# Forgetting attention: copies behind the exponent, rests a step later in every second head, and the causal mask added by VectorE in the score bank

## The chip, the cores and the metric

The kernel runs on one core of one Trainium2 chip. Its engines work side by side, each on its own list of instructions: TensorE (PE in the rows; PEld is its weight load), VectorE (DVE), ScalarE (ACT), GpSimd (POOL) and SyncE (SP), which issues DMAs. They meet at semaphores only: an instruction adds to one when it is done, another engine waits until it has reached a value. The metric is the device time of one execution in microseconds (us); less is better.

## The reference, cut to what matters

The program is two transformer blocks over 512 tokens of 1024 features. The change lies in the forgetting attention of the second block: 8 heads of 64, causal, with the running sum F of log-sigmoids of a gate added to the scores.

```python
F = jnp.cumsum(jax.nn.log_sigmoid(f_logit.astype(jnp.float32)), axis=1).transpose(0, 2, 1)
...
s = jnp.einsum('bhqd,bshd->bhqs', q_blk, k, preferred_element_type=jnp.float32)
s = s + F_blk[..., None] - F[:, :, None, :]
s = jnp.where(pos_blk[:, None] >= k_pos[None, :], s, -jnp.inf)
p = jax.nn.softmax(s, axis=-1).astype(v.dtype)
return jnp.einsum('bhqs,bshd->bqhd', p, v)
```

Everything is computed in float32 to the accuracy of float32: a product is made of three matmuls, of the high part of each operand and of the "rest" (the operand less its rounded high part).

## The kernel before, in words

**Order of the work.** Each engine's order is written out by hand; nothing is scheduled. After the projections (`pe_mix_in`), the attention runs in 32 steps, 8 heads h times 4 blocks qt of 128 queries; step i is head i // 4, block i % 4, and its scores have n = 128, 256, 384 or 512 columns, as block qt sees only keys up to itself. I call the last 128 of these columns the own block; only there does the mask act.

**One step, engine by engine.**

- TensorE (`pe_fox`, L2556) makes the scores of step i in one of three banks (`score_bank`): a matmul of query and key (L2571), a bf16 matmul that adds the mask in the own block (L2572: identity times a matrix with 0 and -1e30), and a matmul with the rests and with F (L2573). Then it transposes the probabilities of step i-3 (L2581, n/128 of them), at a head's first step also multiplies the values of head h-2 (`fox_out`, L2600, 8 of them in a trace row), and last it does a piece of another job: three k-tiles of three matmuls (L2308 to L2310) of the delta-rule projections ("conv products").
- VectorE (`dve_fox`, L2604) takes the negated maximum of each row of scores (L2625), then `inverse_sum` (L2619) of the exponent's sums. Between these it works on the projection tiles: it reads a tile when it is ready (L2338), adds three convolution taps (L2348), and gates it (L2360). For the next head it makes the query's rest (L2438) and the key's rest (L2442), before the change in blocks 0 and 1 of every head from head 1 on.
- ScalarE (`act_fox`, L2673) in step i: copies the turned probabilities of step i-4 from a bank to SBUF (L2682, the "copy"), scales the probabilities of step i-1 (L2686), takes the exponent of step i (L2692), and then serves the projection tiles (L2366, L2371), and rounds queries and keys of the coming head (L2425 to L2449).
- GpSimd (`pool_fox`) splits weights for the projections and builds masks; among them, earlier, the causal mask CM (`pool_causal_mask`).

**What waits for what, around the change.** The transposes of step j = i-3 write one of two banks, so they wait for the copy of step j-2 = i-5 (`fx_pt`). They also wait for the scaled probabilities of step j (`fx_p`). Scores of step i wait for the exponent of step i-3 (`fx_e`), since three banks take turns. A head's first step waits for both rests of that head (`fx_rest`) and for the rounded operands. The exponent waits for the maximum (`fx_nm`), the scaling for the inverse sum (`fx_r`), and VectorE's inverse sum for the exponent.

**Tiles of the projections.** Twelve tiles end in steps 2, 5, 7, 10, 13, 15, 18, ..., three per two heads. A tile is read in that step, its taps are added one step later, and it is gated three steps later. Where VectorE has both in a step, the read or gate stands ahead of what follows, as the code below shows.

Of the kernel before, what the change touches and what calls it, by code (L numbers as in the profile page):

```python
# [20 lines left out]
BF16 = mybir.dt.bfloat16  # L21
# [5 lines left out]
P = 128  # L27
# [118 lines left out]
def _members(kind, *parts):  # L146
# [20 lines left out]
    [("b_xc_lo", KB), ("row_sel", 4), ("f_rows", 1), ("gb_split", 4), ("go_with_q", TOK), ("column_half", 1)], [("b_xc_hi", KB), ("row_ones", 2), ("mask_b", 2), ("f_placed", 4)],  # L167
# [56 lines left out]
def build(nc, dram, out, phases=PHASES, dump=None):  # L224
# [3 lines left out]
    with ctx:  # L228
        base = 16640

        def place(name, at_kib, shape, dt=F32):
            return nc.alloc_sbuf_tensor_at(name, [P] + shape, dt, offset=base + int(at_kib * KIB))
# [1955 lines left out]
        IDENT_B = place("ident_b", ZAT + 28, [P], BF16)  # L2188
        CAUSAL_B = place("causal_b", ZAT + 28.25, [P], BF16)
# [186 lines left out]
        def act_mix_in(act):  # L2376
# [7 lines left out]
            nc.scalar.activation(IDENT_B[:, :], IDENT[:, :], ACT.Copy).then_inc(S("mask_b"), 1)  # L2384
            act.wait_ge(*due("causal", 2))
            nc.scalar.activation(CAUSAL_B[:, :], CM, ACT.Copy).then_inc(S("mask_b"), 1)

# [168 lines left out]
        def pe_fox(pe):  # L2556
            pe.wait_ge(*due("fk", PFQ.rounds - 1))
            pe.wait_ge(*due("mask_b", 2))
            for i in range(STEPS + 2):
                h, qt = divmod(i, TOK)  # L2560
                if i < STEPS:
                    if qt == 0:
                        pe.wait_ge(*due("fx_rowc", h + 1))
                        pe.wait_ge(*due("fx_rest", 2 * h + 2))
                        pe.wait_ge(*due("fx_rounded", query_again(h)))
                        if h == 0:
                            pe.wait_ge(*due("f_placed", 4))
                    n, ps = (qt + 1) * P, score_bank(i)
                    if i >= 3:
                        pe.wait_ge(*due("fx_e", i - 2))  # L2570
                    nc.tensor.matmul(ps[:, 0:n], FX_Q[h % 2][:, qt * P:n], FX_K[h % 2][:, 0, 0:n], start=True, stop=False)  # L2571
                    nc.tensor.matmul(ps[:, n - P:n], IDENT_B[:, :], CAUSAL_B[:, :], start=False, stop=False)  # L2572
                    nc.tensor.matmul(ps[:, 0:n], FX_QF[:, h % 2, qt * P:n], FX_K[h % 2][:, 1, 0:n], start=False, stop=True).then_inc(S("fx_s"), 1)  # L2573
# [30 lines left out]
        def dve_fox(dve, step):  # L2604
            MXC, SUMC = SC[:, 0:32], SC[:, 32:64]

# [13 lines left out]
            for i in range(STEPS + 3):  # L2620
                h, qt = divmod(i, TOK)
                if i < STEPS:
                    n = (qt + 1) * P
                    dve.wait_ge(*due("fx_s", i + 1))
                    nc.vector.reduce_max(MXC[:, i:i + 1], score_bank(i)[:, 0:n], axis=AX.X, negate=True).then_inc(S("fx_nm"), 1)  # L2625
# [14 lines left out]
                if 1 <= h and h + 1 < FOXH and qt == 0:  # L2640
                    dve_query_rest(dve, h + 1)
                elif 1 <= h and h + 1 < FOXH and qt == 1:
                    dve_key_rest(dve, h + 1)
# [29 lines left out]
        def act_fox(act):  # L2673
            MXC, SUMC = SC[:, 0:32], SC[:, 32:64]
            for i in range(STEPS + 3):
                h, qt = divmod(i, TOK)
                for j in turned_at(i - 1) if i else []:
                    jh, jq = divmod(j, TOK)
                    act.wait_ge(*due("fx_t", j + 1))
                    if jh >= 2 and jq == 0:  # L2680
                        act.wait_ge(*due("fx_o", jh - 1))
                    nc.scalar.activation(FPT[:, jh % 2, 0:jq + 1, jq * P:(jq + 1) * P], PS[2 + j % 2][:, 0:(jq + 1) * P].rearrange("p (k q) -> p k q", q=P), ACT.Copy).then_inc(S("fx_pt"), 1)  # L2682
# [4 lines left out]
                if i < STEPS:  # L2687
# [4 lines left out]
                    nc.scalar.activation(FP[:, i % 3, 0:n], score_bank(i)[:, 0:n], ACT.Exp, bias=MXC[:, i:i + 1], accum_out=SUMC[:, i:i + 1]).then_inc(S("fx_e"), 1)  # L2692
                started, ended = tile_at(i, 0), tile_at(i, 2)
# [1099 lines left out]
```

## Time and profile before

| | us |
|---|---|
| median of 3 runs (lowest to highest) | 1822.17 (1821.49 to 1822.44) |
| profiled execution, its own time | 1823.4 |
| its span, first to last instruction | 1821.7 |

| engine | busy us | share of the span |
|---|---|---|
| PE matmul | 1786.6 | 98% |
| DVE | 1175.9 | 65% |
| ACT | 740.6 | 41% |
| POOL | 1310.0 | 72% |

The two stretches of [rows 2] begin and end with the first score matmul of a head (1053.09 is step 4, 1080.78 step 12, 1109.08 step 20). The 32 steps start at 1042.35 (first score matmul) and the last of them ends at about 1155 us of the span. A busy PE is one with a matmul in flight: starts, not durations, tell what one matmul costs the next. A row of the timeline has the start, the duration and the operation, and in brackets how long its engine stood idle before it and who released it.

### The profile page before, as it was taken

The page shows a single profiled execution, that of the slowest core. Times are in us where ns is not written, and L with a number is a line of the kernel's source. Part 1 is how long each engine was busy: PE and PEld are TensorE (multiplying, and loading weights), DVE is VectorE, ACT ScalarE, POOL GpSimd, SP SyncE. Part 2 cuts the span into 40 slices and gives each one's busy share as a digit, 9 for nine tenths or more (in the row PEclk, how much of TensorE's full clock was granted, in tenths as well). Part 3 has the DMA queues.
Part 4 walks back from the last instruction along what each step waited for, and adds up shares of the span by engine and source line. Part 5 has one row for each costly group of instructions (what it writes and reads, how often), then busy time and mean ns, then how long its engine had stood idle before and what let it go on. Part 6 is the DMA issues. An engine that isn't in the chain of part 4 may idle for free.

```text
span 1821.7 us, 28330 instructions
## 1 busy us (share of the span) xinstructions
PE 1786.6 (98%) x10180; PEld 1523.0 (84%) x10180; DVE 1175.9 (65%) x1775; ACT 740.6 (41%) x1386; POOL 1310.0 (72%) x1188
## 2 busy tenths in 40 slices
PE   9999999999999999999999999999999999999998
PEld 7788888878878799998888867798876778999886
DVE  7976664249974798877017777664454189888631
ACT  5521111137762466652014277453413256565001
POOL 8976666767777798877667865453772688888775
PEclk9999999999999999999999999999999999999999
DMA  7022223232123323234222211101321222322421
GB/s 280 1 101 84 92 92 139 92 128 88 73 76 109 139 94 116 94 116 183 95 93 105 105 58 56 61 26 47 116 95 45 93 109 80 113 102 108 168 98 69
DMA packets 26014, 179.36 MB, mean 98 GB/s; under 512 B 2864, under 2 KB 2992, under 8 KB 6960
## 3 DMA queue, kind: packets, MB, share of 16 engines
q1 hardware_dynamic: 24176, 168.31, 25.8%
q10 hardware_dynamic: 1728, 9.58, 1.4%
q8 instruction: 70, 1.15, 0.2%
q14 instruction: 40, 0.33, 0.1%
HBM read 171.58 MB, written 6.29 MB: 98 GB/s over the span
## 4 chain that ended last, share of the span: by engine, by line
PE 82%; DVE 8%; ACT 4%; issue 3%; POOL 3%; DMA 1%; ACTq 0%; DVEq 0%; POOLq 0%
PE bank L484 12%; PE bank L485 12%; PE bank L486 12%; PE bank L1432 6%; PE bank L1433 6%; PE bank L1434 6%; PE bank L1904 2%; PE bank L1902 2%; PE bank L1903 2%; PE bank L522 1%; POOL weights_lo L762 1%; PE bank L524 1%; PE bank L523 1%; DVE x_mixed_lo L1608 1%; PE bank L3183 1%
## 5 line engine op out<-in xcount | busy, mean ns | idle before, releaser
L376 POOL TENSOR_TENSOR weights_lo<-raw_weights,weights_hi 128x512 fp32r<-128x512 f32 (+4 forms) x400 | 543.1, 1358 | 39.8 <-ACT weights_hi L395 7.4
L374 POOL TENSOR_SCALAR weights_hi<-raw_weights 128x512 fp32r<-128x512 f32 (+4 forms) x376 | 259.5, 690 | 314.3 <-PE bank L486 170.6
L484 PE MATMUL bank<-x_hi,weights_hi 128*128 128x512 f32 x688 | 271.5, 395 | 0.2
L486 PE MATMUL bank<-x_lo,weights_hi 128*128 128x512 f32 x688 | 267.9, 389 | 0.0
L485 PE MATMUL bank<-x_hi,weights_lo 128*128 128x512 f32 x688 | 267.8, 389 | 0.0
L484 PEld LDWEIGHTS bank<-x_hi,weights_hi 128*128 128x128 f32 x688 | 129.2, 188 | 28.1 <-POOL weights_lo L376 0.8
L486 PEld LDWEIGHTS bank<-x_lo,weights_hi 128*128 128x128 f32 x688 | 129.1, 188 | 27.1
L485 PEld LDWEIGHTS bank<-x_hi,weights_lo 128*128 128x128 f32 x688 | 129.2, 188 | 27.0 <-issue 1.0
L1434 PE MATMUL bank<-x_lo,weights_hi 128*128 128x256 f32 x432 | 122.4, 283 | 0.0
L1474 POOL TENSOR_TENSOR weights_lo<-temps,weights_hi 128x512 fp32r<-128x512 f32 x72 | 107.5, 1512 | 4.7 <-ACT weights_hi L1511 4.7
L1474 POOL TENSOR_TENSOR weights_lo<-raw_weights,weights_hi 128x512 fp32r<-128x512 f32 x72 | 97.6, 1358 | 13.3 <-ACT weights_hi L1511 13.0
L1432 PE MATMUL bank<-x_mixed_hi,weights_hi 128*128 128x256 f32 x288 | 81.8, 284 | 2.0 <-DVE bank L1697 2.0
L1434 PEld LDWEIGHTS bank<-x_lo,weights_hi 128*128 128x128 f32 x432 | 83.2, 193 | 0.0
L1432 PE MATMUL bank<-x_hi,weights_hi 128*128 128x256 f32 x288 | 82.0, 285 | 0.5 <-ACT temps L1523 0.5
L1433 PE MATMUL bank<-x_hi,weights_lo 128*128 128x256 f32 x288 | 81.8, 284 | 0.0
L1433 PE MATMUL bank<-x_mixed_hi,weights_lo 128*128 128x256 f32 x288 | 81.5, 283 | 0.0
L1474 POOL TENSOR_TENSOR weights_both<-temps,weights_lo 128x512 fp32r<-128x512 f32 x36 | 49.9, 1386 | 33.9 <-ACT weights_lo L1511 33.9
L1628 DVE TENSOR_TENSOR temps<-raw_weights 128x512 f32<-128x512 f32 x71 | 72.4, 1020 | 0.0
L484 PE MATMUL bank<-ffn_y_hi,weights_hi 128*128 128x512 f32 x176 | 68.8, 391 | 0.0
L486 PE MATMUL bank<-ffn_y_lo,weights_hi 128*128 128x512 f32 x176 | 68.5, 389 | 0.0
L485 PE MATMUL bank<-ffn_y_hi,weights_lo 128*128 128x512 f32 x176 | 68.5, 389 | 0.0
L1902 PE MATMUL bank<-weights_hi,ffn_y_hi 128*128 128x512 f32 x176 | 68.5, 389 | 0.0
(588 smaller groups left out, 5186.3 us busy)
## 6 DMA issues: line engine op xcount, KB each, us to landing
raw_weights<-in_ffn_seven SPq DMA_DIRECT2D x36, 1024.0 KB, 4.7
raw_weights<-in_a_ug SPq DMA_DIRECT2D x16, 1024.0 KB, 4.8
raw_weights<-in_b_in SPq DMA_DIRECT2D x12, 1024.0 KB, 4.7
raw_weights<-in_ffn_down SPq DMA_DIRECT2D x12, 1024.0 KB, 4.7
raw_weights<-in_ffn_down SPq DMA_DIRECT2D x7, 1408.0 KB, 6.1
raw_weights<-in_a_out SPq DMA_DIRECT2D x8, 1024.0 KB, 4.8
raw_weights<-in_ffn_up SPq DMA_DIRECT2D x8, 1024.0 KB, 4.8
raw_weights<-in_b_out SPq DMA_DIRECT2D x8, 768.0 KB, 4.2
```

What stands on the lines that cost most here:

```text
L374: nc.gpsimd.tensor_scalar(hi, raw, 1.0, 0.0, ALU.mult, ALU.add).then_inc(S("units_hi"), 1)
L376: nc.gpsimd.tensor_tensor(lo, raw, hi.bitcast(F32), ALU.subtract).then_inc(units_ready, 1)
L484: nc.tensor.matmul(ps, wh, xh[:, k, :], start=k == 0, stop=False)
L485: nc.tensor.matmul(ps, wl, xh[:, k, :], start=False, stop=False)
L486: last = nc.tensor.matmul(ps, wh, xl[:, k, :], start=False, stop=k == last_k)
L1432: nc.tensor.matmul(out, wh, xh(k), start=opens and k == 0, stop=False, skip_group_check=True)
L1433: nc.tensor.matmul(out, wl, xh(k), start=False, stop=False, skip_group_check=True)
L1434: last = nc.tensor.matmul(out, wh, xl(k), start=False, stop=k == 3, skip_group_check=True)
L1474: nc.gpsimd.tensor_tensor(RING_LO[p], source_of(r, p), RING_HI[p].bitcast(F32), ALU.subtract).then_inc(S("seven_lo"), 1)
L1628: nc.vector.tensor_tensor(sum_of(p), x, y, op).then_inc(S("seven_sums"), 1)
L1902: nc.tensor.matmul(bank, Y_H[:, k, tok], wh, start=k == 0, stop=False)
L1903: nc.tensor.matmul(bank, Y_H[:, k, tok], wl, start=False, stop=False)
```

## The change

Four things are done, all inside the attention:

1. The bf16 mask matmul of each of the 32 steps is gone, and with it the bf16 copies of identity and mask (two ScalarE copies, made some 45 us ahead of the first step).
2. VectorE instead adds the mask CM, in float32, to the own block in the score bank (128 x 128), ahead of the row maximum; the maximum waits for this add through the new semaphore count `fx_masked`. All scores of a bank are then complete as before.
3. ScalarE makes the copy of turned probabilities right behind the exponent: in step i that of step i-3, where before it was made at the head of step i+1.
4. In heads 2, 4 and 6 the rests of the next head are made one block later, in blocks 1 and 2 (`later` = 1); in heads 1, 3 and 5 they stay in blocks 0 and 1.

```diff
@@ act_mix_in
-            nc.scalar.activation(IDENT_B[:, :], IDENT[:, :], ACT.Copy).then_inc(S("mask_b"), 1)
-            act.wait_ge(*due("causal", 2))
-            nc.scalar.activation(CAUSAL_B[:, :], CM, ACT.Copy).then_inc(S("mask_b"), 1)
@@ pe_fox
-            pe.wait_ge(*due("mask_b", 2))
...
                     nc.tensor.matmul(ps[:, 0:n], FX_Q[h % 2][:, qt * P:n], FX_K[h % 2][:, 0, 0:n], start=True, stop=False)
-                    nc.tensor.matmul(ps[:, n - P:n], IDENT_B[:, :], CAUSAL_B[:, :], start=False, stop=False)
                     nc.tensor.matmul(ps[:, 0:n], FX_QF[:, h % 2, qt * P:n], FX_K[h % 2][:, 1, 0:n], start=False, stop=True).then_inc(S("fx_s"), 1)
@@ dve_fox
+            dve.wait_ge(*due("causal", 2))
...
+                    own_block = score_bank(i)[:, n - P:n]
                     dve.wait_ge(*due("fx_s", i + 1))
+                    nc.vector.tensor_tensor(own_block, own_block, CM, ALU.add).then_inc(S("fx_masked"), 1)
+                    dve.wait_ge(*due("fx_masked", i + 1))
                     nc.vector.reduce_max(MXC[:, i:i + 1], score_bank(i)[:, 0:n], axis=AX.X, negate=True).then_inc(S("fx_nm"), 1)
...
-                if 1 <= h and h + 1 < FOXH and qt == 0:
+                later = 1 - h % 2
+                if 1 <= h and h + 1 < FOXH and qt == later:
                     dve_query_rest(dve, h + 1)
-                elif 1 <= h and h + 1 < FOXH and qt == 1:
+                elif 1 <= h and h + 1 < FOXH and qt == 1 + later:
                     dve_key_rest(dve, h + 1)
@@ act_fox
             for i in range(STEPS + 3):
                 h, qt = divmod(i, TOK)
-                for j in turned_at(i - 1) if i else []:
-                    ... (wait for fx_t and fx_o, copy to FPT)
                 if 1 <= i <= STEPS:
...
                     nc.scalar.activation(FP[:, i % 3, 0:n], score_bank(i)[:, 0:n], ACT.Exp, bias=MXC[:, i:i + 1], accum_out=SUMC[:, i:i + 1]).then_inc(S("fx_e"), 1)
+                for j in turned_at(i):
+                    ... (the same waits and the same copy)
```

**ScalarE around the exponent of step 13** (head 3, block 1: the row with 128x256 from a bank). Before:

```order
L2434 ACTIVATE fox_q_with_f<-fox_q 64x512
L2682 ACTIVATE fox_pt<-bank 128x2x128
L2686 ACTIVATE fox_p<-fox_p,scratch_cols 128x128
L2692 ACTIVATE fox_p,scratch_cols<-bank,scratch_cols 128x256
L2366 ACTIVATE temps<-gdn_xb_a,vecs 128x512
L2449 ACTIVATE fox_q_with_f<-fox_f_queries,head_selectors 64x512
L2430 ACTIVATE fox_k_even<-fox_k 64x512
L2682 ACTIVATE fox_pt<-bank 128x3x128
L2686 ACTIVATE fox_p<-fox_p,scratch_cols 128x256
```

The same stretch after the change, with its new line numbers (L2684 is the exponent, L2690 the copy, L2678 the scaling):

```order
L2429 ACTIVATE fox_q_with_f<-fox_q 64x512
L2678 ACTIVATE fox_p<-fox_p,scratch_cols 128x128
L2684 ACTIVATE fox_p,scratch_cols<-bank,scratch_cols 128x256
L2690 ACTIVATE fox_pt<-bank 128x3x128
L2364 ACTIVATE temps<-gdn_xb_a,vecs 128x512
L2444 ACTIVATE fox_q_with_f<-fox_f_queries,head_selectors 64x512
L2425 ACTIVATE fox_k_even<-fox_k 64x512
L2678 ACTIVATE fox_p<-fox_p,scratch_cols 128x256
```

The copy of three tiles (step 10) has moved from behind the work for tile and head to right behind the exponent; the number of copies is the same.

**VectorE in head 2, from the taps of step 8 to the maximum of step 11** (`fox_q_odd` is the query's rest for head 3, `fox_k_odd` the key's). Before:

```order
L2348 SCALAR_TENSOR_TENSOR temps<-gdn_xb_a,vecs,temps 128x512 x3
L2438 TENSOR_TENSOR fox_q_odd<-fox_q,fox_q_odd 64x512
L2625 TENSOR_REDUCE scratch_cols<-bank 128x1
L2619 RECIPROCAL scratch_cols<-scratch_cols 128x1
L2442 TENSOR_TENSOR fox_k_odd<-fox_k,fox_k_odd 64x512
L2625 TENSOR_REDUCE scratch_cols<-bank 128x1
L2360 SCALAR_TENSOR_TENSOR gdn_qkv_t<-gdn_qkv_t,temps 128x512
L2619 RECIPROCAL scratch_cols<-scratch_cols 128x1
L2338 TENSOR_TENSOR gdn_xb_b<-bank,rms_rows 128x512
L2625 TENSOR_REDUCE scratch_cols<-bank 128x1
```

The same stretch after the change (L2620 is the mask's add, L2622 the maximum, L2613 the inverse, L2433 and L2437 the rests):

```order
L2346 SCALAR_TENSOR_TENSOR temps<-gdn_xb_a,vecs,temps 128x512 x3
L2620 TENSOR_TENSOR bank<-bank,masks 128x128
L2622 TENSOR_REDUCE scratch_cols<-bank 128x1
L2613 RECIPROCAL scratch_cols<-scratch_cols 128x1
L2433 TENSOR_TENSOR fox_q_odd<-fox_q,fox_q_odd 64x512
L2620 TENSOR_TENSOR bank<-bank,masks 128x128
L2622 TENSOR_REDUCE scratch_cols<-bank 128x1
L2358 SCALAR_TENSOR_TENSOR gdn_qkv_t<-gdn_qkv_t,temps 128x512
L2613 RECIPROCAL scratch_cols<-scratch_cols 128x1
L2336 TENSOR_TENSOR gdn_xb_b<-bank,rms_rows 128x512
L2437 TENSOR_TENSOR fox_k_odd<-fox_k,fox_k_odd 64x512
L2620 TENSOR_TENSOR bank<-bank,masks 128x128
```

An add stands ahead of each maximum; the query's rest has gone behind the maximum and inverse of step 9, and the key's rest behind everything of step 10, which makes it the last piece ahead of step 11.

## Rows read from the trace of the kernel before

**Rows 1.** The page: the span, and the chain that ended last by engine.

```profile
span 1821.7 us, 28330 instructions
PE 82%; DVE 8%; ACT 4%; issue 3%; POOL 3%; DMA 1%; ACTq 0%; DVEq 0%; POOLq 0%
```

**Rows 2.** Stretches: length, PE, PEld, DVE, ACT, POOL busy (count), granted clock, DMA.

```profile
1053.09:1080.78 27.69, 25.04 (x125) 18.79 (x124) 22.65 (x37) 18.10 (x44) 18.18 (x20) 1.00 0.15 50
1080.78:1109.08 28.30, 27.41 (x134) 19.93 (x132) 19.51 (x36) 21.76 (x50) 15.98 (x20) 1.00 0.17 64
```

**Rows 3.** Waits of TensorE, 1042 to 1158: total us, times, longest.

```profile
PE bank L2581 <- ACT fox_pt L2682: 4.6, 5, 1.6
```

**Rows 4.** Waits of TensorE behind the attention, 1158 to 1330.

```profile
PE bank L2799 <- DVE temps L2804: 0.2, 1, 0.2
```

**Rows 5.** Groups by form, 1042 to 1158: count, busy us, mean ns, idle before.

```profile
L2572 PE MATMUL bank<-causal_b,ident_b 128*128 128x128 bf16 x32 | 7.4, 230 | 0.0
```

**Rows 6.** Timeline of TensorE and its weight loads, step 15.

```profile
1092.72 0.40 PE L2571 MATMUL bank<-fox_k_odd,fox_q_odd 128*128 128x512 f32 x1
1092.95 0.10 PEld L2572 LDWEIGHTS bank<-causal_b,ident_b 128*128 128x128 bf16 x1 [0.28 <-issue]
1092.96 0.23 PE L2572 MATMUL bank<-causal_b,ident_b 128*128 128x128 bf16 x1
1092.96 0.20 PEld L2573 LDWEIGHTS bank<-fox_k_odd,fox_q_with_f 128*128 128x128 f32 x1
1093.00 0.48 PE L2573 MATMUL bank<-fox_k_odd,fox_q_with_f 128*128 128x512 f32 x1
1093.31 0.27 PE L2581 MATMUL bank<-ident,fox_p 128*128 128x128 f32 x1
```

**Rows 7.** Timeline of TensorE: transposes that waited in steps 11, 12 and 20.

```profile
1078.59 0.30 PE L2581 MATMUL bank<-ident,fox_p 128*128 128x128 f32 x1 [1.57 <-ACT fox_pt L2682]
1082.08 0.41 PE L2581 MATMUL bank<-ident,fox_p 128*128 128x128 f32 x2 [0.89 <-ACT fox_pt L2682]
...
1110.02 0.41 PE L2581 MATMUL bank<-ident,fox_p 128*128 128x128 f32 x2 [0.54 <-ACT fox_pt L2682]
```

**Rows 8.** Timeline of ScalarE: exponent 9, the copy, exponents 10 and 18.

```profile
1075.72 0.47 ACT L2692 ACTIVATE fox_p<-bank,scratch_cols 128x256 f32<-128x256 f32 x1 [2.73 <-DVE scratch_cols L2625]
...
1077.98 0.47 ACT L2682 ACTIVATE fox_pt<-bank 128x384 f32<-128x384 f32 x1
...
1078.88 0.56 ACT L2692 ACTIVATE fox_p<-bank,scratch_cols 128x384 f32<-128x384 f32 x1
...
1107.18 0.56 ACT L2692 ACTIVATE fox_p<-bank,scratch_cols 128x384 f32<-128x384 f32 x1
```

**Rows 9.** Timeline of VectorE in steps 8 to 10.

```profile
1073.70 1.66 DVE L2438 TENSOR_TENSOR fox_q_odd<-fox_q,fox_q_odd 64x512 fp32r<-64x512 f32 x1
1075.28 0.41 DVE L2625 TENSOR_REDUCE scratch_cols<-bank 128x1 f32<-128x256 f32 x1
...
1076.52 0.69 DVE L2442 TENSOR_TENSOR fox_k_odd<-fox_k,fox_k_odd 64x512 fp32r<-64x512 f32 x1
1077.24 0.56 DVE L2625 TENSOR_REDUCE scratch_cols<-bank 128x1 f32<-128x384 f32 x1
...
1079.57 0.16 DVE L2619 RECIPROCAL scratch_cols<-scratch_cols 128x1 f32<-128x1 f32 x1 [0.69 <-ACT fox_p L2692]
1080.00 0.69 DVE L2338 TENSOR_TENSOR gdn_xb_b<-bank,rms_rows 128x512 f32<-128x512 f32 x1 [0.27 <-issue]
```

**Rows 10.** Groups of VectorE by form, 1042 to 1152.

```profile
L2625 DVE TENSOR_REDUCE scratch_cols<-bank 128x1 f32<-128x512 f32 x8 | 5.5, 684 | 0.7 <-PE bank L2573 0.7
L2338 DVE TENSOR_TENSOR gdn_xb_a<-bank,rms_rows 128x512 f32<-128x512 f32 x6 | 4.1, 690 | 0.9 <-PE bank L2310 0.8
L2438 DVE TENSOR_TENSOR fox_q_odd<-fox_q,fox_q_odd 64x512 fp32r<-64x512 f32 x3 | 3.6, 1212 | 0.1
L2625 DVE TENSOR_REDUCE scratch_cols<-bank 128x1 f32<-128x128 f32 x8 | 2.2, 280 | 0.0
```

More of the change, by code:

```diff
@@ L166 @@
     *(_members(kind, ("fx", FOXH * TOK), ("ma", MH * TOK)) for kind in ("s", "nm", "e", "p", "t", "pt")),
-    [("b_xc_lo", KB), ("row_sel", 4), ("f_rows", 1), ("gb_split", 4), ("go_with_q", TOK), ("column_half", 1)], [("b_xc_hi", KB), ("row_ones", 2), ("mask_b", 2), ("f_placed", 4)],
+    [("b_xc_lo", KB), ("row_sel", 4), ("f_rows", 1), ("gb_split", 4), ("go_with_q", TOK), ("column_half", 1)], [("b_xc_hi", KB), ("row_ones", 2), ("f_placed", 4), ("fx_masked", FOXH * TOK)],
     [("beta_tanh", 1), ("a_exp", 1), ("rows_exp", 1)],
@@ L2187, in build @@
         HEAD_SEL = place("head_selectors", 207.53125, [FOXH])
-        IDENT_B = place("ident_b", ZAT + 28, [P], BF16)
-        CAUSAL_B = place("causal_b", ZAT + 28.25, [P], BF16)
         FP = place("fox_p", ZAT + 2, [3, SEQ])
@@ L2676, in act_fox @@
                 h, qt = divmod(i, TOK)
-                for j in turned_at(i - 1) if i else []:
[L2678 to L2682, printed above, removed]
                 if 1 <= i <= STEPS:
@@ L2692, in act_fox @@
                     nc.scalar.activation(FP[:, i % 3, 0:n], score_bank(i)[:, 0:n], ACT.Exp, bias=MXC[:, i:i + 1], accum_out=SUMC[:, i:i + 1]).then_inc(S("fx_e"), 1)
+                for j in turned_at(i):
+                    jh, jq = divmod(j, TOK)
+                    act.wait_ge(*due("fx_t", j + 1))
+                    if jh >= 2 and jq == 0:
+                        act.wait_ge(*due("fx_o", jh - 1))
+                    nc.scalar.activation(FPT[:, jh % 2, 0:jq + 1, jq * P:(jq + 1) * P], PS[2 + j % 2][:, 0:(jq + 1) * P].rearrange("p (k q) -> p k q", q=P), ACT.Copy).then_inc(S("fx_pt"), 1)
                 started, ended = tile_at(i, 0), tile_at(i, 2)
```

## The prediction

> **What bounds the kernel now.** The page first: the chain that ended last runs through TensorE for 82% of the 1821.7 us span, VectorE and ScalarE have 8% and 4% [rows 1]. So this edit pays only as far as TensorE's stream gets shorter or waits less. Next the stretches of the attention: in steps 4 to 11 TensorE is busy 25.04 of 27.69 us and VectorE 22.65, in steps 12 to 19 it is 27.41 of 28.30 and 19.51, at the full granted clock in both [rows 2]. The reader is to see a TensorE with few holes, and a VectorE that has little room in the first of the two stretches. The table of waits names the holes: five times, 4.6 us in all, transposes waited for the copy of turned probabilities, the longest 1.6 us [rows 3]. The timeline puts one in step 11 (1.57), one in step 12 (0.89) and one in step 20 (0.54) [rows 7]; the other two, in steps 7 and 28, share what is left, 4.6 - 3.0 = 1.6 us. Behind the attention TensorE waits next to nothing for VectorE (0.2 us) [rows 4].
>
> Why the copy is late in step 11: exponent 9 starts at 1075.72, having waited 2.73 us for its maximum; ScalarE then serves tile and head and comes to the copy at 1077.98, and the transposes start at 1078.59 [rows 7, 8]. The maximum was late because VectorE first made the query's rest, 1.66 us from 1073.70 on [rows 9].
>
> **Part 1, the mask matmul removed.** 32 are gone. Their busy time is 230 ns each, 7.4 us in all [rows 5], but matmuls overlap, and starts count. In step 15 L2572 starts at 1092.96 and L2573 at 1093.00: 0.04 us. L2573 itself then holds on for 0.31 until the next start, where L2571 of the same 512 columns took 0.24 (1092.72 to 1092.96) [rows 6]; its duration is 0.08 longer too (0.48 against 0.40). I read this as a weight load (0.20) that the short mask matmul cannot cover. Without the mask matmul it lies beside L2571: at 512 and 384 columns all of it (0.04 + 0.08 = 0.12 saved), at 256 about half (0.09, an interpolation), at 128 columns none (0.04). Mean 0.09 us per step. Bounds: 0.04, the start distance alone, and 0.23, the busy time. For the 20 steps from 12 on: 1.9 us, between 0.8 and 4.6. The two ScalarE copies that go lie some 45 us earlier, where ScalarE idles: nothing.
>
> The Trainium skill, page "TensorE: Matmul & The Clock Gate", Part 3, The mechanism, says that a weight load overlaps with matmuls in flight only where the row groups differ; for full-height tiles the mask's own load (0.10) would then be exposed too, and each step would give some 0.15. The trace disagrees: the 0.20 load of L2573 starts at 1092.96 and its matmul 0.04 later [rows 6]. By the page the 20 steps would give 3.0 instead of 1.9.
>
> **Part 2, the add on VectorE.** No row shows a 128 x 128 add in a bank. The maximum of 128 columns takes 280 ns and of 512 columns 684; a tensor-tensor of bank and SBUF at 512 columns takes 690, much the same [rows 10]. So I take 0.28 for the add, plus 0.04 until the dependent maximum starts, an estimate: 0.32 us per step, 10.2 us of VectorE in 32 steps, 2.6 per two heads. Bounds: 0.15 (the maximum's fixed part, 280 less 128 columns at (684 - 280)/384 ns) and 0.69. VectorE's load in steps 12 to 19 rises from 19.5 to 22.1 of some 27 us; below TensorE, but all of the add lies on the chain score, maximum, exponent, inverse sum. Queued behind it on VectorE are reads, taps and rests, for which ScalarE and TensorE wait.
>
> A tensor-tensor can be stretched by GpSimd: the odd query rest took 1.66 in head 2, 1.21 on the mean, the read of a tile (one operand in a bank) 690 [rows 9, 10]. The Trainium skill, page "SBUF — State Buffer", section "SBUF: two separate sides", gives the reason: a VectorE instruction with two SBUF inputs and GpSimd lock each other out of one pair of ports for a whole instruction. The add has one input in the bank, so by that rule it is not stretched, while the moved rest can be. If it were stretched as the rest is (1.66/0.69), it would be 0.67 and 12 us more of VectorE.
>
> **Part 3, the copy moved.** It is needed two TensorE steps after its exponent is issued instead of one. In step 11 the copy of step 6 follows exponent 9, which ends near 1075.0 by the count below, so the 1.57 hole goes. The same for steps 12, 20 and 28. A wait costs its idle time plus 0.17: unhindered, transposes start 0.31 after L2573, that is 0.17 before it ends [rows 6]. What is next to be late is the exponent itself and, at a head's first step, the rests.
>
> **Part 4, the rests moved, and what TensorE finds at step 12.** Take VectorE's own clock; the taps of step 8 end about 1073.7 [rows 9]. Then:
> - add 0.32 and maximum 0.42 come first: exponent 9 starts at 1074.44, not 1075.72.
> - ScalarE from exponent 9 to 10: 3.16 us before (1078.88 - 1075.72, the copy among it) [rows 8]; the same work in another order gives 1077.6. VectorE's side: inverse sum at 1075.1, the query's rest 1.66 to 1076.8, add and maximum 0.88 to 1077.7. Both sides meet: exponent 10 at 1077.7.
> - from exponent 10 to its inverse sum 0.69 (1079.57 - 1078.88), to the read 0.43, the read 0.69: 1079.5. Now the key's rest, 0.69: 1080.2 [rows 8, 9].
>
> TensorE may start step 12 only then, at about 1080.3. It started at 1080.78 before, and its transposes at 1082.08 after their hole; now they follow 0.25 after the start, at 1080.5 [rows 2, 7]. So all that steps 1 to 11 gain on TensorE (the holes of steps 7 and 11, eleven mask matmuls) is cut down by a new wait to **1.6 us**, counted behind step 12. The key's rest stands here with nothing behind it to hide it.
>
> Steps 13 to 31 after that: the holes of steps 20 and 28 go, the second taken to be like the first, 2 x (0.54 + 0.17) = **1.4**. Mask matmuls **1.9**. Against it, the key rests of heads 5 and 7: exponent 18 started 1109.08 - 1107.18 = 1.90 ahead of step 20 [rows 2, 8], and from an exponent to the end of the key's rest it is 0.69 + 0.43 + 0.69 + 0.69 = 2.50. If the chain keeps its distance to TensorE, each such step waits 0.60; if the query's rest, now behind the maximum, lets exponents 17 and 18 come 0.6 earlier, nothing. I take the middle, 0.3 twice: **-0.6**. The adds (+0.32 in each of steps 16 to 18) and the rest out of their way (about -1.0) nearly cancel, which is why I don't take the better end.
>
> **Sum:** 1.6 + 1.4 + 1.9 - 0.6 = 4.3 us. All later work is handed from engine to engine, and it starts from TensorE's last tiles, so it moves along. The profiled execution would go from 1823.4 to 1819.1; it stood 1.2 above the median of its runs, so against the median of 1822.17 the forecast is 1817.9. A difference under 0.2%, 3.6 us, is what a measurement of this kernel can't tell from none.
>
> **Rivals.**
> - B, no rest is late. VectorE's part of the chain is quicker than I count (taps not stretched by GpSimd). Then all five holes go, 4.6 + 5 x 0.17 = 5.4, and 31 mask matmuls at 0.09, 2.8: 8.2 us, 1814.0. For it: the hand-over in step 12 is a matter of 1 to 2 us. Against it: VectorE's 22.65 busy of 27.69 before any add.
> - C, slower: the key's rest of heads 3, 5 and 7 becomes the pace-maker. It stands behind exponent, inverse and read of the step; if an add costs 0.69 (its upper bound) or the moved rest and taps are stretched by GpSimd as in head 2 (1.66), each of the three steps 12, 20 and 28 waits 2 us more than I took, 6 us in all: 4.3 - 6 = -1.7, 1823.9. It decides from about 1.4 us per head pair on. Against it: exponents 9 and 17 lose a rest from ahead of them, and VectorE idles 8.8 us of 28.3 in steps 12 to 19 [rows 2].
> - D, the attention ends sooner but the next part gives it back: TensorE there nearly meets VectorE (the wait of 0.2 us [rows 4]), and if VectorE's key norms end no earlier than now, the gain is lost: 1822. Against it: VectorE's last read waits for TensorE's last tile, so both move.
>
> **How the numbers follow.** Forecast 0.52, B 0.20, C 0.11, D 0.17. The forecast's own range is 1816.4 to 1819.8 (the mask matmul's bounds from 0.8 to 4.6, the rests' waits from 0 to 1.2), about two thirds of it beyond 3.6 us. Faster by over 0.2%: 0.52 x 0.65 + 0.20 = 0.54. Slower by over 0.2%: C beyond its middle, 0.07. Within: 0.39. The range reaches to B below and to D above, a little beyond each for the bounds: 1813.6 to 1822.6.
>
> **What would show it.** The step from L2571 to its partner: 0.24 at 512 columns, and the partner no longer longer than its like. No wait of TensorE for the copy (`fox_pt`), but at step 12 one for VectorE's `fox_k_odd`, of 1 to 3 us, and short or none at 20 and 28. Adds of 0.28 us, constant. Query rests of head 3 behind the maximum of step 9. Exponent 9 over a microsecond earlier against the taps of step 8. Wrong it would be if holes for the copy stay, if TensorE waits for exponents or scaled probabilities, if an add takes over 0.5, or if L2573 keeps its 0.48 without the mask matmul.

## The result and the profile after

After the change the kernel takes 1827.58 us (median of 21 runs), before 1822.21 (21 runs beside them). The medians are 5.4 us apart; the ratio is 1.0021 (3.8 us), with a 95% interval of 1.0015 to 1.0028. The ratio leaves out one run of the changed kernel, in a slow state at 3587.61 us. The forecast was 1817.9 and its range ended at 1822.6, so it was wrong in sign. The profiled execution took 1826.85 (span 1825.1), 3.4 more than that of before.

The page of the profile: TensorE's share of the chain is larger than before [rows 1], but it holds matmuls at the lower clock too.

```profile
span 1825.1 us, 28296 instructions
PE 86%; DVE 6%; POOL 3%; ACT 2%; issue 2%; DMA 1%; ACTq 0%; DVEq 0%; POOLq 0%
```

The three largest waits of TensorE from 1035 to 1180 (us in total, times, longest). The five waits for the copy [rows 3] have become two. Three others stand ahead of `L2565`, a step's first score matmul. They are laid to "issue", which names no releaser; VectorE's timeline below shows that the key's rest ends just ahead of step 12.

```profile
PE bank L2565 <- issue: 6.5, 3, 3.0
PE bank L2574 <- ACT fox_pt L2690: 1.9, 2, 1.5
PE bank L2565 <- DVE fox_k_even L2437: 0.6, 1, 0.6
```

TensorE's timeline gives their places: steps 8 (two), 12, 20 and 28.

```profile
1064.37 0.30 PE L2565 MATMUL bank<-fox_k_even,fox_q_even 128*128 128x128 f32 x1 [0.64 <-DVE fox_k_even L2437]
1066.29 0.46 PE L2574 MATMUL bank<-ident,fox_p 128*128 128x128 f32 x2 [1.51 <-ACT fox_pt L2690]
1084.46 0.30 PE L2565 MATMUL bank<-fox_k_odd,fox_q_odd 128*128 128x128 f32 x1 [2.78 <-issue]
1111.72 0.30 PE L2565 MATMUL bank<-fox_k_odd,fox_q_odd 128*128 128x128 f32 x1 [0.76 <-issue]
1141.53 0.37 PE L2565 MATMUL bank<-fox_k_odd,fox_q_odd 128*128 128x128 f32 x1 [3.00 <-issue]
```

The stretches of [rows 2]: steps 4 to 11 and 12 to 19. TensorE is busy 26.21 of 31.55 us, VectorE 27.54 (22.65 before), and the clock is below 1 in the first.

```profile
1052.91:1084.46 31.55, 26.21 (x117) 19.13 (x116) 27.54 (x45) 20.11 (x46) 20.25 (x24) 0.95 0.20 68
1084.46:1111.72 27.26, 26.50 (x124) 19.87 (x125) 22.81 (x44) 20.72 (x49) 13.78 (x18) 1.00 0.12 39
```

VectorE from the taps of step 8 to the add of step 11 (compare [rows 9]). The key's rest ends at 1084.37, and TensorE's step 12 starts 0.09 later. The order is the one foreseen; everything stands 4 us later than foreseen.

```profile
1073.85 3.66 DVE L2346 SCALAR_TENSOR_TENSOR temps<-gdn_xb_a,vecs,temps 128x512 f32<-128x512 f32 x3
1077.43 0.29 DVE L2620 TENSOR_TENSOR bank<-bank,masks 128x128 f32<-128x128 f32 x1
1077.75 0.42 DVE L2622 TENSOR_REDUCE scratch_cols<-bank 128x1 f32<-128x256 f32 x1
...
1079.00 1.36 DVE L2433 TENSOR_TENSOR fox_q_odd<-fox_q,fox_q_odd 64x512 fp32r<-64x512 f32 x1
...
1082.14 0.69 DVE L2336 TENSOR_TENSOR gdn_xb_b<-bank,rms_rows 128x512 f32<-128x512 f32 x1
1082.87 1.50 DVE L2437 TENSOR_TENSOR fox_k_odd<-fox_k,fox_k_odd 64x512 fp32r<-64x512 f32 x1
1084.40 0.30 DVE L2620 TENSOR_TENSOR bank<-bank,masks 128x128 f32<-128x128 f32 x1
```

VectorE by form, 1042 to 1156 (compare [rows 10]): the add is 292 ns. Work with one operand in a bank has kept its time (read 690, now 684). The key's rest, with two operands in SBUF, takes 1323 ns on the mean of four, 936 before. Not all such work is longer: 34 taps took 31.7 us before and 33 take 32.1 now. What differs is which instruction is stretched, and it is now the rests that TensorE waits for.

```profile
L2620 DVE TENSOR_TENSOR bank<-bank,masks 128x128 f32<-128x128 f32 x31 | 9.1, 292 | 5.8 <-PE bank L2566 5.4
L2437 DVE TENSOR_TENSOR fox_k_odd<-fox_k,fox_k_odd 64x512 fp32r<-64x512 f32 x4 | 5.3, 1323 | 0.1
L2336 DVE TENSOR_TENSOR gdn_xb_a<-bank,rms_rows 128x512 f32<-128x512 f32 x6 | 4.1, 684 | 0.5 <-PE bank L2308 0.5
```

The granted clock, after the change. The first row is the whole of step 8 (0.80). The second lies in it, behind its wait, where the head's output matmuls run almost wholly at the lower level (0.52; 0.50 is 1.2 GHz). The third is the wait ahead of step 28, still at 1.00, and the fourth the same matmuls behind it, at 0.50.

```profile
1064.37:1072.76 8.39, 6.88 (x21) 3.75 (x22) 7.29 (x13) 4.85 (x12) 3.70 (x6) 0.80 0.08 32
1068.00:1070.00 2.00, 2.00 (x4) 0.69 (x3) 1.90 (x5) 0.09 (x1) 0.36 (x1) 0.52 0.00 0
1139.00:1141.00 2.00, 0.00 (x0) 0.00 (x0) 1.83 (x4) 1.65 (x5) 1.80 (x2) 1.00 0.98 414
1142.00:1145.00 3.00, 3.00 (x7) 1.01 (x7) 2.78 (x6) 1.67 (x4) 0.00 (x0) 0.50 0.00 0
```

**The balance.** From the start of step 0 to that of step 31 TensorE took 107.90 us before and takes 112.87, +4.97. Without any wait it is 102.26 with the mask matmuls (the experiment with C, R, the key's rest first, the row splits later and the mask by matmul). Without them it would be 31 x 0.115 less, 98.7; this is an estimate, and the 0.115 is worked out below. So before lost 5.6 and after loses 14.2. By place, each against the same step where nothing waits: the start of step 8 0.8; step 8 itself 3.4 (its wait 1.51 + 0.17, the clock the other 1.7); the starts of steps 12 and 20 3.5 and 0.9; the start of step 28 3.5 and the clock behind it 1.6. That is 13.7 of the 14.2.

Of the 5.0 lost, the two spans show 3.4. Behind the attention, the execution profiled before the change had its own stretch at the lower clock: the same matmuls took 15.85 us there and 12.75 after. The rest behind it took 1.5 us more after (586.15 and 587.62). First before, then after:

```profile
1219.70:1235.55 15.85, 14.89 (x143) 14.31 (x139) 4.33 (x8) 7.71 (x13) 0.00 (x0) 0.78 0.01 1
```

```profile
1224.73:1237.48 12.75, 11.74 (x142) 11.17 (x139) 4.33 (x8) 7.71 (x13) 0.00 (x0) 1.00 0.01 1
```

So the difference of the two spans holds one execution's luck with the clock. The ratio's 3.8 us and the medians' 5.4 lie on either side of the stage's 5.0.

### The profile page after: what moved, and what is told of

Read it like the earlier page. It is cut to its first block, busy times and chain, and to the rows that moved or that the text cites. A ratio compares the mean times of both kernels' runs of the same rounds, so it can differ in the third digit from the quotient of the medians.

```text
span 1825.1 us, 28296 instructions
## 1 busy us (share of the span) xinstructions
PE 1787.0 (98%) x10148; PEld 1523.9 (83%) x10148; DVE 1187.4 (65%) x1807; ACT 740.1 (41%) x1384; POOL 1308.5 (72%) x1188
## 3 DMA queue, kind: packets, MB, share of 16 engines
q8 instruction: 70, 1.15, 0.3%
## 4 chain that ended last, share of the span: by engine, by line
PE 86%; DVE 6%; POOL 3%; ACT 2%; issue 2%; DMA 1%; ACTq 0%; DVEq 0%; POOLq 0%
PE bank L484 12%; PE bank L486 12%; PE bank L485 12%; PE bank L1432 6%; PE bank L1433 6%; PE bank L1434 6%; PE bank L1902 2%; PE bank L1903 2%; PE bank L1904 2%; PE bank L522 1%; PE bank L524 1%; PE bank L523 1%; POOL weights_lo L762 1%; PE bank L2306 1%; PE bank L2593 1%
```

## The experiments

A time is a median; a ratio is to runs of the kernel before on the same chip, with its 95% interval, which reaches some 1.6 to 2.6 us to either side. "C", "R" and "M" are parts 3 (copies), 4 (rests), and 1 with 2 (mask), made by the diff shown ahead. "Lower clock" in a step means that its granted clock was below 1. Distances to the kernel after are of medians; by the ratio that kernel stands 1.6 us lower.

**One part alone, or two of the three.** Edits: only the hunks of the parts named.

```
C: act_fox: -  for j in turned_at(i - 1) if i else []:   (ahead of the scaling)
            +  for j in turned_at(i):                    (behind the exponent)
R: dve_fox: +  later = 1 - h % 2
            -  ... qt == 0: query rest   ... qt == 1: key rest
            +  ... qt == later           ... qt == 1 + later
M: pe_fox:  -  nc.tensor.matmul(ps[:, n - P:n], IDENT_B, CAUSAL_B, ...)
   dve_fox: +  nc.vector.tensor_tensor(own_block, own_block, CM, ALU.add)
```

> The kernel before with part 3 alone: the copy of turned probabilities behind the exponent; mask matmul and rests as before. Theory 1 (the loss is made by the key's rest, which came last in its step behind an add): the five holes of 4.6 us go and nothing takes their place, 1817 to 1818, no wait of TensorE for fox_k_odd. Rival (moving the copy itself delays exponents or scaled probabilities, on which TensorE then waits): 1821 or more, with waits for fox_p or fox_e.

C: 1821.51, 0.9994 (0.9985 to 1.0003). Neither theory: the five waits became one of 3.1 us, again for the copy, in step 11, with the lower clock behind it.

> The changed kernel with its rests back in blocks 0 and 1 of every head: copies and mask add only. Theory 1 (the later rests make the waits of 2.8, 0.8 and 3.0 us): these waits go, 1817 to 1819. Theory 2 (32 adds on VectorE make every chain late, wherever the rests stand): TensorE waits elsewhere for about as long, for scores' exponents or the query's rest, 1824 or more.

C, M: 1822.85, 0.9998 (0.9989 to 1.0007), between the two theories. No wait for the key's rest at steps 12, 20 and 28, but seven for the copy from step 8 on, 6.4 us in all, and the lower clock in step 8.

> The kernel before with parts 1 and 2 alone: mask matmul removed, add on VectorE; copies and rests as before. A matmul is worth 0.11 us a step by the traces, 3.4 us in 32. Theory 1: the holes for the copy stay and grow by less than what the matmuls give, 1820 to 1822. Theory 2: each add of 0.32 on the chain to the exponent makes the copy later still, holes of 8 to 12 us, 1824 to 1828.

M: 1828.26, 1.0032 (1.0022 to 1.0043); transposes wait 11.2 us for the copy, as theory 2 had it.

> The kernel before with part 4 alone: rests one block later in heads 2, 4 and 6. Theory 1: exponents 9 and 10 start a microsecond sooner, the copy in step 11 too, and the key's rest ends at about 1080.1 of the trace where step 12 starts near 1079.5 if the hole of 1.57 is gone: a wait of 0.5 to 1.5 at steps 12, 20 and 28, 1821 to 1823. Rival (the rests are only harmful together with adds, alone they help): 1819 to 1820, no wait for fox_k_odd.

R: 1819.14, 0.9978 (0.9969 to 0.9987), as the rival had it.

> The kernel before with parts 3 and 4: copies behind the exponent and rests later, the mask matmul kept, no add on VectorE. The runs so far: copies alone 0.9994, rests alone 0.9978 of before. Theory A (the adds are what makes the later rests late): no wait of TensorE for the key's rest above 0.5 us, no hole for the copy, 1817 to 1819. Theory 1 as it stood (the later key rest alone makes the waits): waits of 1 us and more at steps 12, 20 and 28, 1820 to 1823.

C, R: 1822.48, 1.0000 (0.9991 to 1.0009), the time of theory 1, but of its three waits only that at step 12.

> Parts 1, 2 and 4: mask add on VectorE, rests later, the copy where it was. Mask alone had a hole of 3.0 us for the copy at steps 12 and 20 and ran at 1.0032. Theory A: the copy is late again by the adds, since nothing else moved it; the rests later give back some 3 us of it, 1824 to 1827. Rival (copy and rests each help alone, whatever stands beside): 1822.

R, M: 1824.50, 1.0009 (1.0000 to 1.0018), as theory A had it.

The parts don't add: C gives 1 us at most (its interval reaches to none), R 3 to 4, both together nothing. M alone costs 5.5. The trace of C with R has the long wait at step 12 already without an add, and it stands behind taps of 3.64 and a key's rest of 1.49 us. Its waits of TensorE, then its VectorE:

```profile
PE bank L2571 <- issue: 2.8, 1, 2.8
PE bank L2581 <- ACT fox_pt L2693: 1.4, 1, 1.4
```

```profile
1071.95 3.64 DVE L2348 SCALAR_TENSOR_TENSOR temps<-gdn_xb_a,vecs,temps 128x512 f32<-128x512 f32 x3
...
1080.61 1.49 DVE L2442 TENSOR_TENSOR fox_k_odd<-fox_k,fox_k_odd 64x512 fp32r<-64x512 f32 x1
```

With R alone TensorE comes to step 8 1.2 us later, counted from step 0, as it had waited for a copy in step 7. The same instructions take 2.54 and 0.69, and the wait at step 12 is 0.2. (Step 0 starts at 1044.29 in this trace, in that of C with R at 1042.24.)

```profile
1073.41 2.54 DVE L2348 SCALAR_TENSOR_TENSOR temps<-gdn_xb_a,vecs,temps 128x512 f32<-128x512 f32 x3
...
1080.96 0.69 DVE L2442 TENSOR_TENSOR fox_k_odd<-fox_k,fox_k_odd 64x512 fp32r<-64x512 f32 x1
```

**The mask matmul taken out, no add in its place** (C, R; leaves out the causal mask inside a row's own block).

```
-  nc.tensor.matmul(ps[:, n - P:n], IDENT_B, CAUSAL_B, ...)
```

> The same, and the mask matmul left out without an add in its place; this kernel leaves the causal mask out in a query block's own 128 columns. It is the changed kernel less its 32 adds. By the starts in the changed kernel's trace a mask matmul takes 0.11 us: 3.4 us less than copies and rests with the matmul, 1814 to 1815.5. The distance from here to the changed kernel is then what the adds cost: theory A expects 10 us or more, with two clock falls of TensorE among them. Rival: the matmuls were covered by waits and this is within 1 us of copies and rests.

1819.85, 0.9984 (0.9975 to 0.9993), 4 to 6 us above the expectation; 2.6 us under C with R. That is what leaving out the 32 matmuls gives here; the wait of 2.8 at step 12 and the lower clock behind it are still there. The kernel after, which has the adds besides, takes 7.7 more (10 or more was expected).

**GpSimd's low parts left out in the attention** (kernel after; leaves out the low parts of those projection weights, which keep old values).

```
-  nc.gpsimd.tensor_tensor(lo, raw, hi, ALU.subtract)
+  nc.gpsimd.memset(lo[:, 0, 0:1], 0.0)        (one column; gdn_qkv and gdn_z only)
```

> The changed kernel, with GpSimd's subtraction for the low weight part left out in the units of the attention (the low part keeps old values, so the projection tiles are not the reference's). It takes the one GpSimd instruction with two SBUF inputs from beside the taps and rests. Theory B (VectorE's two-SBUF instructions are stretched by GpSimd, taps 1043 ns and key rests 1323 ns on the mean): taps fall to 0.75 to 0.8, rests to 0.7, the waits of 2.8 and 3.0 us at steps 12 and 28 shrink below 1 us, 1816 to 1819. Rival (the stretching is made by GpSimd's other work, or costs nothing that TensorE sees): taps stay near 1 us and the time above 1823.

1817.31, 0.9974 (0.9964 to 0.9984), 10 us under the kernel after. Taps of step 8 and the key's rest, against 3.66 and 1.50; the add stays at 0.3:

```profile
1071.12 2.31 DVE L2349 SCALAR_TENSOR_TENSOR temps<-gdn_xb_a,vecs,temps 128x512 f32<-128x512 f32 x3
...
1078.78 0.81 DVE L2440 TENSOR_TENSOR fox_k_odd<-fox_k,fox_k_odd 64x512 fp32r<-64x512 f32 x1
```

So GpSimd's subtraction is what stretched these. It isn't the only one: in this trace two rests still take 0.98 and 0.99 us, each begun 0.36 to 0.39 us after GpSimd's rounding of the weights (`TENSOR_SCALAR`, 0.81 and 0.84 us).

Two things in this trace bear on the prediction. The taps of step 8 end at 1073.43 and the key's rest at 1079.59, where it had counted 1073.7 and 1080.2. So its clock of VectorE comes out where the taps aren't stretched, though not term by term (it had 1.66 for the query's rest, which takes 0.69 here). And the wait ahead of step 12 is still 2.10 us, where the expectation had below 1, with the lower clock in that step: the rest is late here at 0.81 us already, and stretching only makes it later. That 1817.31 lies near the forecast of 1817.9 shows nothing more, as the subtraction was never left out of the kernel before, and no run here tells what it costs there.

**The key's rest right behind the maximum** (kernel after).

```
   nc.vector.reduce_max(...)
+  if 1 <= h and h + 1 < FOXH and qt == 1 + later: dve_key_rest(dve, h + 1)
   ...   (gate, inverse sum, read, taps)
-  elif ... qt == 1 + later: dve_key_rest(dve, h + 1)
```

> The changed kernel with each key's rest made right behind the maximum of its step, ahead of gate, inverse sum and read, where the exponent runs beside it. Theory 1 (the key rest is late at steps 12, 20 and 28 because it stands last in its step, behind exponent, inverse and read): the waits for fox_k_odd fall from 2.8, 0.8 and 3.0 to below 1 us each, 1821 to 1824. Theory C (VectorE as a whole is behind at step 12, by stretched taps and split rows in steps 4 to 8): another wait comes in its place, for copy or query's rest, and the time stays within 2 us of the changed kernel.

1820.01, 0.9988 (0.9979 to 0.9997): 7.6 us under the kernel after (6.0 by the ratios), by the place of one instruction in six steps. No wait for a key's rest is left at steps 12, 20 and 28; what waits there are now lie in step 8 (for the rounded key and for the copy, with the lower clock) and for the copy in steps 16, 19 and 20.

```profile
PE bank L2574 <- ACT fox_pt L2690: 3.3, 4, 1.1
PE bank L2565 <- ACT fox_k_even L2425: 1.4, 1, 1.4
```

**VectorE's row splits moved.** These four short instructions (`split_rows`) have nothing to do with the change; they stand in steps 3 to 6, in the first of the two stretches, where VectorE has less room.

```
-  if 3 <= i < 7: split_rows(i - 3)
+  if 20 <= i < 24: split_rows(i - 20)
```

> The changed kernel with the four instructions that split the gate rows moved from steps 3 to 6 to steps 20 to 23 (nothing needs them before the attention ends). They took 3.5 us and more of VectorE in the stretch where it was busiest. Theory C: the holes at steps 8, 11 and 12 go mostly (1.5, 0.4 and 2.8 us) and with them the clock fall of step 8, those of step 28 stay: 1821 to 1824. Theory 1: step 12 still waits 2 to 3 us for the key's rest, over 1825.

Kernel after: 1823.70, 1.0010 (1.0001 to 1.0020). Step 8 starts without a wait, at 1063.24; the starts of steps 12, 20 and 28 keep waits (1.42, 1.35 and 2.78; at step 12 half of what it was). So the time and the wait of step 8 go with theory C, and what is left at step 12 lies between the two.

> Rests later alone (which ran at 0.9978), and the row splits moved to steps 20 to 23. It had a wait of 1.1 us for the copy at step 7 and 0.4 more. Theory C: these go, 1817.5 to 1818.5. Rival: VectorE's phase against GpSimd shifts and taps collide elsewhere: 1819 to 1821.

R: 1819.21, 0.9980 (0.9971 to 0.9989), no change against R alone: the waits at step 7 and 11 are gone, and one of 1.3 us for the copy came in step 27.

> Copies behind the exponent and rests later, mask matmul kept (ran at 1.000, with holes of 1.4 and 2.8 us at steps 11 and 12 and a clock fall behind them), and the row splits moved to steps 20 to 23. Theory C: holes and clock fall go, some 6 us less, 1816 to 1817.5, the fastest that keeps the mask. Rival (the 3.6 us taps of step 8 alone make the holes): 1820 to 1822.

C, R: 1816.32, 0.9965 (0.9951 to 0.9978), 6 us under C with R, as theory C had it. The waits of C with R in step 11 (1.45) and ahead of step 12 (2.78), and the lower clock in step 12, are gone; one of 0.55 at step 28 is left. So together the two parts do give more than R alone, once VectorE has room in steps 3 to 6.

**The price of the add once no rest is late.** Edits as above, put together ("both moves": the key's rest first and the row splits later); and, in the kernel after, every add made twice.

> The changed kernel with both moves: the key's rest right behind the maximum, and VectorE's four row splits in steps 20 to 23 instead of 3 to 6. Theory A (VectorE's lateness at head starts is the whole cause, and adds are free once it is gone): the two moves take away 7.6 us (key rest) and about 3.9 (splits, 1823.7 against 1827.6), partly the same wait, so about 1816, no wait at steps 12, 20 and 28 over 0.5 us. Theory B (the adds have a price of their own, on the chain score, maximum, exponent): 1819 to 1821, as with the key rest alone, with waits for probabilities or their copy left.

C, R, M with both moves: 1819.82, 0.9984 (0.9975 to 0.9993). No wait for a rest and no step at the lower clock, but six waits for the copy, as theory B had it:

```profile
PE bank L2574 <- ACT fox_pt L2690: 4.7, 6, 1.3
```

> Copies and rests moved, the key's rest right behind the maximum, mask still by TensorE's matmul. Against the changed kernel with the key's rest there (1820.0) only the mask differs. Theory A: the matmuls cost 0.107 us x 31 = 3.3 us and the adds nothing, so 1823 or a little more. Theory B: the adds cost more than the matmuls give, so under 1820: 1816 to 1818, with no wait left at step 12.

C, R, key's rest first: 1820.54, 0.9985 (0.9976 to 0.9994), level with the same and M (1820.01). Neither theory: A had 1823 for it, B 1816 to 1818.

> The same with the row splits in steps 20 to 23. Without the move of the key's rest it took 1816.3, with one wait of 0.6 us (plus one at step 28, 0.7 by the starts). Both theories: 1815 to 1816. What it tells apart: against the changed kernel with both moves, only the mask differs. Theory A: that one is 3.3 us faster than this. Theory B: this one is faster or they are level.

C, R with both moves, mask by matmul: 1816.59, 0.9966 (0.9954 to 0.9978), 3.2 us under the same with M; theory A had that one 3.3 faster. Steps 4 to 11 and 12 to 19 of it; TensorE is busy throughout at the full clock:

```profile
1053.07:1077.78 24.71, 24.71 (x126) 18.85 (x124) 19.47 (x34) 19.28 (x45) 16.67 (x20) 1.00 0.12 44
1077.78:1104.95 27.17, 27.17 (x133) 19.89 (x132) 20.14 (x36) 21.32 (x51) 15.41 (x20) 1.00 0.22 78
```

> The changed kernel with each add of the causal mask made twice (masked scores go further below, the probabilities stay zero): 32 more adds of 0.29 us, 0.33 on the chain. Theory A (adds lengthen only the way to the three late key rests): from step 8 to 12 some 4 more adds, 4 x 0.33 = 1.3 us per head pair, 3 to 4 us in all: 1831. Theory B (each add is paid on the chain): 32 x 0.33 = 10.5 us, 1838. If VectorE had room: 1828, as with one add.

1837.72, 1.0080 (1.0066 to 1.0094), 10.1 us over the kernel after, with 32 adds of 0.30 more. TensorE's waits:

```profile
PE bank L2565 <- issue: 8.7, 3, 3.0
PE bank L2574 <- ACT fox_pt L2692: 4.1, 5, 1.2
PE bank L2565 <- ACT fox_k_even L2425: 1.1, 1, 1.1
```

The total is what theory B gave (32 x 0.33 = 10.5 us), but the trace doesn't show it paid add by add. Steps 13 to 18 take the same time with two adds as with one (18.64 and 18.62 us). Of the 9.6 us that TensorE is longer from step 0 to 31, 9.4 lie at the four heads' starts, in steps 7 and 8, 11 and 12, 19 and 20, 27 and 28. The waits shown there grew from 9.0 to 13.9, most of them for a rest, and the lower clock, which makes most of the remainder, stands behind more of them (steps 8, 12, 20 and 28, where it was 8 and 28). So the waits are those of theory A, at a price that it had not counted, and the agreement with theory B's number is in part luck.

What M costs, by pairs that differ in it alone, in us:

| beside | medians | ratios |
|---|---|---|
| the kernel before | 5.5 | 5.8 |
| C | 1.3 | 0.7 |
| R | 5.4 | 5.6 |
| C, R | 5.1 | 3.8 |
| C, R, row splits later | 7.4 | 8.2 |
| C, R, key's rest first | -0.5 | 0.5 |
| C, R, both moves | 3.2 | 3.3 |

Each is uncertain by 2 to 3 us, so the rows of C and of the key's rest first can't be told from nothing; but none shows the gain of 3 us that TensorE's own stream would give. Theory A (the adds are free once no rest is late) falls with the last pair. There no wait for a rest is left in either kernel, and the one with M waits 4.7 us for copies, which fits theory B: an add is paid on the chain score, maximum, exponent, copy. The traces give the same difference for that pair, 105.35 against 102.26 us from step 0 to 31. The pair with the key's rest first and the splits in place is level. It has a wait for the rounded key in the kernel with M (1.4 us) and three for the copy in the other, and what makes it level stays open.

## Why the prediction was wrong, step by step

- **TensorE bounds, what counts is its waits:** right. Without waits in the attention the kernel takes 1816.6 with the mask matmuls in it. It left out that matmuls at the lower clock can follow a wait.
- **Part 1, the matmul's worth:** right, a little small. Two kernels without waits in steps 8 to 11 take 13.59 us with it and 13.13 without, 0.115 a step (I took 0.09); by width 0.07, 0.12, 0.14, 0.13 at 128 to 512 columns, where I had 0.04, 0.09, 0.12, 0.12. The reading of the weight load fits: in step 15 of the kernel after the partner starts 0.22 behind the first and takes 0.39, not 0.48 [rows 6].

```profile
1095.02 0.39 PE L2565 MATMUL bank<-fox_k_odd,fox_q_odd 128*128 128x512 f32 x1
1095.24 0.39 PE L2566 MATMUL bank<-fox_k_odd,fox_q_with_f 128*128 128x512 f32 x1
```

- **Part 2, the add:** its size was right (292 ns, constant, 0.33 to the maximum), its cost wrong. "Below TensorE" was said of VectorE's load, and the sum prices the add only on the way to the heads' starts. But the add lies on chains that TensorE waits for: with both moves it costs 3.2 us more than the matmuls that it replaces, and a second add 10.1.
- **Part 3, the copies:** the holes of steps 7, 11, 12, 20 and 28 went, apart from 0.4 in step 11. A new one of 1.51 came in step 8, where I had looked for none; a hole for the copy was one of the signs of being wrong.
- **Part 4, step 12: the step that failed is "Take VectorE's own clock; the taps of step 8 end about 1073.7".** I kept that instant from the trace of before, as if nothing ahead of it moved. It was 1077.51 (1073.85 + 3.66). From there to the end of the key's rest I counted 6.5 and it took 6.86. The instant came 3.84 late (before, it was 1073.67). Step 8 starts 1.07 earlier but is 3.33 longer, by the wait of 1.51 + 0.17 and the lower clock. The chain ahead of the taps gives 0.5 more (the add of step 8 is in it), and the taps themselves are 1.08 longer.
- What made step 8 wait lies in step 6. VectorE in that step, after the change: the gate took 1.83, the row split 1.45. The exponent of step 6 and the copy behind it, for which step 8 waits, are ScalarE's:

```profile
1059.47 1.83 DVE L2358 SCALAR_TENSOR_TENSOR gdn_qkv_t<-gdn_qkv_t,temps 128x512 f32<-128x512 f32 x1
...
1061.29 0.67 DVE L2336 TENSOR_TENSOR gdn_xb_b<-bank,rms_rows 128x512 f32<-128x512 f32 x1
1061.99 1.45 DVE L2605 TENSOR_SCALAR gdn_split_rows<-token_rows 4x512 fp32r<-4x512 f32 x1
1063.47 0.68 DVE L2437 TENSOR_TENSOR fox_k_even<-fox_k,fox_k_even 64x512 fp32r<-64x512 f32 x1
...
1064.99 0.58 ACT L2684 ACTIVATE fox_p<-bank,scratch_cols 128x384 f32<-128x384 f32 x1 [0.34 <-DVE scratch_cols L2622]
...
1065.56 0.59 ACT L2690 ACTIVATE fox_pt<-bank 128x512 f32<-128x512 f32 x1
```

Before, the gate took 0.68 there and the row split 0.62:

```profile
1058.94 0.68 DVE L2360 SCALAR_TENSOR_TENSOR gdn_qkv_t<-gdn_qkv_t,temps 128x512 f32<-128x512 f32 x1
...
1060.44 0.62 DVE L2611 TENSOR_SCALAR gdn_split_rows<-token_rows 4x512 fp32r<-4x512 f32 x1
1061.09 1.10 DVE L2442 TENSOR_TENSOR fox_k_even<-fox_k,fox_k_even 64x512 fp32r<-64x512 f32 x1
```

The key's rest of head 2 ends 2 us later than before: the adds give 0.5, the gate 1.15, the row split 0.83, and the rest itself is 0.4 shorter. Exponent 6 starts at 1064.99 instead of 1063.38, and the copy behind it comes too late for step 8. With the row splits moved the wait of step 8 is gone, and so it is nearly (0.44 is left) without GpSimd's subtraction; each of the two was needed for it.

- **-0.6 for heads 5 and 7:** the second term that failed. The starts of steps 20 and 28 waited 0.76 and 3.00, not 0.3 each. Ahead of step 20 the key's rest took 0.69, and the 0.76 is near the 0.60 that I had if the chain keeps its distance. Ahead of step 28 both rests are stretched, the query's to 1.67 and the key's to 1.44:

```profile
1135.86 1.67 DVE L2433 TENSOR_TENSOR fox_q_odd<-fox_q,fox_q_odd 64x512 fp32r<-64x512 f32 x1
...
1139.99 1.44 DVE L2437 TENSOR_TENSOR fox_k_odd<-fox_k,fox_k_odd 64x512 fp32r<-64x512 f32 x1
```

- **The forecast's own range** was mis-added: with the bounds that it names it is 1814.6 to 1819.6, not 1816.4 to 1819.8. The measured time lies above either.
- **Rival C had the mechanism:** the key's rest of heads 3, 5 and 7 as the pace-maker, by the second of its two conditions (rest and taps stretched by GpSimd). The stretching came at steps 12 and 28 and not at 20. It was priced at 1823.9, without the lower clock (3.3 us) and the wait of step 8. I gave it 0.11, because "exponents 9 and 17 lose a rest from ahead of them"; the add and longer taps took that place. The idle 8.8 us of VectorE in steps 12 to 19 were no argument for steps 8 to 12 and 24 to 28.
- **B fell:** in the changed kernel, to have no late rest takes the key's rest moved ahead. **D fell:** behind the attention both kernels run alike (69.45 and 69.31 us for the first part), apart from the clock.

## What to carry to other kernels

When an engine falls behind only in some steps, count those steps from where all the steps before them put it, not from instants of the old trace. An instruction that one engine sheds and another takes on is worth its time only if the first engine doesn't wait for the second one's chain. Double it to see what it costs, and look in the trace where: here the total fitted one theory and the places another. Where another engine waits at its next step for one instruction of this step, that instruction should not stand last; here its place was worth 7.6 us by the medians, 6.0 by the ratios.

## What the runs showed of the hardware

- A VectorE instruction with two operands in SBUF takes up to 1.67 us instead of 0.69 (a gate 1.83) when GpSimd's subtraction began ahead of it, and three taps 3.66 instead of 2.31. Where VectorE's began no later, it is GpSimd's that is longer: 1.81 us instead of 1.27 beside the key's rest of 0.69 in [rows 9]. The first row is before, the second after, where the rest that begins 0.32 later takes 1.50:

```profile
1076.52 1.81 POOL L376 TENSOR_TENSOR weights_lo<-raw_weights,weights_hi 128x512 fp32r<-128x512 f32 x1
```

```profile
1082.55 1.27 POOL L376 TENSOR_TENSOR weights_lo<-raw_weights,weights_hi 128x512 fp32r<-128x512 f32 x1
```

- Adds of 292 ns and reads of 684, with an operand in a bank, were never stretched. GpSimd starts a piece of weights when TensorE has left one (after the change, the rounding ahead of the second row had waited 2.03 us for TensorE), so which instruction of VectorE is hit moves with TensorE. C with R against R alone is the case: TensorE 1.2 us earlier, taps 1.1 and a rest 0.8 us longer. The Trainium skill, page "SBUF — State Buffer", section "SBUF: two separate sides", has the rule for two SBUF inputs; these rows agree. The row split, with one SBUF input (1.45 against 0.62 us), is stretched as well, which the page allows for an instruction in a 2-port performance mode; no run here tells its mode.
- The granted clock falls to 1.2 GHz behind some waits and not behind others. In the kernel after it fell behind 1.51 us in step 8 and behind 3.00 ahead of step 28, and did not behind 2.78 ahead of step 12; in C with R it did fall behind 2.78 at that same step (0.75 over the step). Each fall in the kernel after cost 1.6 to 1.7 us. Its runs bunch: six at 1821.2 to 1824.4, thirteen at 1826.6 to 1829.0, and one at 1831.0. Only one run, in the upper bunch, has a trace here, so whether the falls make the two bunches stays open.
